# Attention pair loop: value product into its own pair, later key blocks summed before one product, tail copies one unit earlier

## The reference, cut to what matters

```python
z = jnp.einsum('bhtd,bhsd->bhts', qb, kb) * scale
mask = (s_idx[None, :] < t_idx[:, None]) & (s_idx[None, :] >= pad)
log_beta = jax.nn.log_sigmoid(z)
log_rest = jnp.where(mask, jax.nn.log_sigmoid(-z), 0.0)
later = lax.cumsum(log_rest, axis=3, reverse=True) - log_rest
att = jnp.where(mask, jnp.exp(log_beta + later), 0.0)
out = jnp.einsum('bhts,bhsd->bhtd', att, vb)
```

## Time and profile before

| what | us |
|---|---|
| median of three runs | 1735.72 |
| the profiled execution | 1740.51 |
| its span, first to last instruction | 1738.4 |
| TensorE busy in the span | 1616.3 |
| a steady pair of attention (156.15 to 189.67) | 33.52 |
| the last pair (290.21 to 326.92) | 36.71 |

### The profile page before, as it was taken

One profiled execution on the slowest core, in us unless ns is written; L12 is line 12 of the kernel. 1 busy time (PEld: TensorE's weight loads), 2 busy tenths in 40 slices (PEclk: granted clock), 3 DMA queues, 4 the chain that ended last, 5 costly groups with the idle time before them and its releaser, 6 DMA issues. The chain is left out here.

```text
span 1738.4 us, 35740 instructions
## 1 busy us (share of the span) xinstructions
PE 1616.3 (93%) x16180; PEld 1459.7 (84%) x16180; DVE 810.9 (47%) x1098; ACT 610.9 (35%) x827; POOL 162.9 (9%) x186
## 2 busy tenths in 40 slices
PE   4999998899999999979999979888669999999997
PEld 3999987899999999979998968887438888888885
DVE  3455445154442344456766535445485444334432
ACT  2445435242221222236567332233243333122321
POOL 2001001001100011300000321101030010001100
PEclk9999999799999999998999979999889999999998
DMA  3221120122332233332222110000103333323331
GB/s 100 68 62 44 56 64 30 49 86 87 97 105 78 86 89 103 97 116 79 81 70 60 45 52 4 5 4 4 49 22 87 95 90 112 91 86 97 96 99 49
DMA packets 214167, 121.35 MB, mean 70 GB/s; under 512 B 8744, under 2 KB 209600, under 8 KB 213760
## 3 DMA queue, kind: packets, MB, share of 16 engines
q1 hardware_dynamic: 213712, 118.98, 23.3%
q10 hardware_dynamic: 304, 0.08, 0.0%
HBM read 112.29 MB, written 6.76 MB: 68 GB/s over the span
## 5 line engine op out<-in xcount | busy, mean ns | idle before, releaser
L125 ACT ACTIVATE w_hi<-w_raw 128x1024 fp32r<-128x1024 f32 (+1 forms) x194 | 215.9, 1114 | 600.0 <-PE psg L732 481.0
L732 PE MATMUL psg<-x_hi,w_hi 128*128 128x264 f32 (+1 forms) x1096 | 357.2, 326 | 9.3 <-PEq L2469 9.3
L732 PE MATMUL psg<-x_lo,w_hi 128*128 128x264 f32 (+1 forms) x1096 | 357.2, 326 | 0.0
L732 PE MATMUL psg<-x_hi,w_lo 128*128 128x264 f32 (+1 forms) x1096 | 356.4, 325 | 0.0
L129 DVE TENSOR_TENSOR w_lo<-w_raw,w_hi 128x1024 fp32r<-128x1024 f32 (+1 forms) x194 | 250.4, 1291 | 145.5 <-ACT w_hi L125 145.5
L732 PEld LDWEIGHTS psg<-x_hi,w_hi 128*128 128x128 f32 x1096 | 206.2, 188 | 28.8 <-issue 10.3
L732 PEld LDWEIGHTS psg<-x_lo,w_hi 128*128 128x128 f32 x1096 | 206.2, 188 | 18.1 <-issue 0.2
L732 PEld LDWEIGHTS psg<-x_hi,w_lo 128*128 128x128 f32 x1096 | 206.6, 189 | 17.5
L732 PE MATMUL psg<-mid_hi,w_hi 128*128 128x264 f32 (+1 forms) x451 | 146.5, 325 | 0.0
L732 PE MATMUL psg<-mid_lo,w_hi 128*128 128x264 f32 (+1 forms) x451 | 146.3, 324 | 0.0
L732 PE MATMUL psg<-mid_hi,w_lo 128*128 128x264 f32 (+1 forms) x451 | 145.9, 323 | 0.0
(11 more groups left out here) (367 smaller groups left out, 3370.6 us busy)
## 6 DMA issues: line engine op xcount, KB each, us to landing
w_raw<-in_w_ffn_in_dram SPq DMA_DIRECT2D x88, 512.0 KB, 3.8
w_raw<-in_w_ffn_out_dram SPq DMA_DIRECT2D x32, 704.0 KB, 4.6
w_raw<-in_w_qkv_dram SPq DMA_DIRECT2D x24, 512.0 KB, 3.7
w_raw<-in_w_rkv_dram SPq DMA_DIRECT2D x24, 512.0 KB, 3.8
w_raw<-in_w_o_attn_dram SPq DMA_DIRECT2D x8, 512.0 KB, 4.1
w_raw<-in_w_o_rwkv_dram SPq DMA_DIRECT2D x8, 512.0 KB, 3.8
v_first<-v_pair SPq DMA_DIRECT2D x8, 264.0 KB, 2.1
res_kept<-res SPq DMA_DIRECT2D x1, 2112.0 KB, 7.8
```

The lines of the kernel that those rows point to most:

```text
L125: k.nc.scalar.activation(k.w_hi[j][:, 0:kt, :], k.raw[j][:, 0:kt, :], ACT.Copy).then_inc(k.hi_ready[j].h, 1)
L732: done = k.nc.tensor.matmul(k.psg[:, 2 * j + c, 0:size], w[:, t, :], x, start=t == first and n == 0, stop=t == last and n == 2)
```

## The change

In the attention: the product of v (unit 3p+2) moves from the previous pair's gaps to just behind `z(p)`, so each pair computes its own v; q and k of the next pair move one and two places back, with the second half of k right before the next `z`. All units from 2 on use one pair of PSUM banks. `later` is split: `own_block` is the triangular part; the cross part (`later_blocks`) no longer multiplies every pair of blocks. Instead VectorE adds the later key blocks' log-rests up in place, from the last block backwards (`later_keys`: 16, 144 and 272 columns, each waiting for the one before), ScalarE and VectorE split these sums (864 columns) into high and low (`sums_high`, `sums_low`), and TensorE makes four cross products per head, high and low. VectorE's and ScalarE's programs are reordered to match. In the tail, ScalarE's copies move from behind m = 5 to behind m = 4.

```diff
     def banks(self, i):
-        if i == 2:
-            return k.psx[:, 2, 0:HALF], k.psg[:, 2, 0:HALF]
         return k.psg[:, 3, 0:HALF], k.psx[:, 3, 0:HALF]
...
+        def sums_high(p, hp):
+            act.wait_ge(self.add_r.h, 3 * (2 * p + hp + 1))
+            if p:
+                act.wait_ge(self.later_d.h, 2 * (p - 1) + hp + 1)
+            nc.scalar.activation(b.sum_hi[hp][:], b.rest[hp][:, 512:SCORES], ACT.Copy).then_inc(self.shi_r.h, 1)
...
         for p in range(PAIRS):
-            unit_hi(k, act, 3 * p + 4, KT)
+            unit_hi(k, act, 3 * p + 3, KT)
...
             rest_high(p, 1, 1)
-            if not last:
-                unit_hi(k, act, 3 * p + 5, KT)
+            sums_high(p, 0)
+            sums_high(p, 1)
+            unit_hi(k, act, 3 * p + 4, KT)
             attend(p, 0)
             attend(p, 1)
             if not last:
-                unit_hi(k, act, 3 * p + 6, KT)
+                unit_hi(k, act, 3 * p + 5, KT)
...
+        def later_keys(p, hp):
+            n = 2 * p + hp
+            at = [piece_cols(a).start for a in (1, 3, 4, 5)]
+            dve.wait_ge(self.rlo_far.h, n + 1)
+            for step, (to, width, skip) in enumerate(((2, 16, 128), (1, 144, 128), (0, 272, 128))):
+                if step:
+                    dve.wait_ge(self.add_r.h, 3 * n + step)
+                own = b.rest[hp][:, at[to] + skip:at[to] + skip + width]
+                nc.vector.tensor_tensor(own, own, b.rest[hp][:, at[to + 1]:at[to + 1] + width], ALU.add)\
+                    .then_inc(self.add_r.h, 1)
+
+        def sums_low(p, hp):
+            dve.wait_ge(self.shi_r.h, 2 * p + hp + 1)
+            nc.vector.tensor_tensor(b.sum_lo[hp][:], b.rest[hp][:, 512:SCORES], b.sum_hi[hp][:].bitcast(F32),
+                                    ALU.subtract).then_inc(self.slo_r.h, 1)
...
-        unit_lo(k, dve, 3, KT)
-        evict(2, 0)
-        evict(2, 1)
         for p in range(PAIRS):
-            unit_lo(k, dve, 3 * p + 4, KT)
+            unit_lo(k, dve, 3 * p + 3, KT)
             clip(p, 0, 0)
...
             softplus(p, 0, 0)
+            evict(3 * p + 2, 0)
+            softplus(p, 0, 1)
+            evict(3 * p + 2, 1)
+            softplus(p, 1, 0)
+            rest_low(p, 0)
+            later_keys(p, 0)
+            softplus(p, 1, 1)
+            rest_low(p, 1)
+            later_keys(p, 1)
+            sums_low(p, 0)
+            sums_low(p, 1)
             if not last:
                 evict(3 * p + 3, 0)
...
+            unit_lo(k, dve, 3 * p + 4, KT)
             if not last:
                 evict(3 * p + 3, 1)
...
+                unit_lo(k, dve, 3 * p + 5, KT)
+                evict(3 * p + 4, 0)
...
+                evict(3 * p + 4, 1)
...
+        def later_blocks(p, hp):
+            ps = (k.psg, k.psx)[hp]
+            pe.wait_ge(self.slo_r.h, 2 * p + hp + 1)
+            for a, c in ((0, 1), (1, 3), (3, 4), (4, 5)):
+                bank, col, width, key, t0 = PIECES[a]
+                _, _, width2, _, t2 = PIECES[c]
+                at, cols = col + t2 - t0, piece_cols(c)
+                for r in (b.sum_hi[hp], b.sum_lo[hp]):
+                    done = mm(ps[:, bank, at:at + width2], b.minus[:], r[:, cols.start - 512:cols.stop - 512], start=False,
+                              stop=True, skip_group_check=True)
             done.then_inc(self.later_d.h, 1)
...
-        half(2, 0)
-        half(2, 1)
         for p in range(PAIRS):
             fill = p < PAIRS - 1
             z(p)
+            half(3 * p + 2, 0)
+            half(3 * p + 2, 1)
             if fill:
                 half(3 * p + 3, 0)
+            own_block(p, 0)
+            own_block(p, 1)
+            later_blocks(p, 0)
+            later_blocks(p, 1)
+            if fill:
                 half(3 * p + 3, 1)
-                half(3 * p + 4, 0)
-            later(p, 0)
-            later(p, 1)
-            if fill:
-                half(3 * p + 4, 1)
             turn_v(p)
             if fill:
-                half(3 * p + 5, 0)
+                half(3 * p + 4, 0)
             values(p)
             if fill:
-                half(3 * p + 5, 1)
+                half(3 * p + 4, 1)
...
-            if m == 5:
+            if m == 4:
                 act.wait_ge(self.turned.h, 1)
                 for g in range(GROUPS):
                     nc.scalar.activation(b.tok[:, g, 0:D // 2], k.psx[:, g, :], ACT.Copy).then_inc(self.copied.h, 1)
```

More of the change, by code:

```diff
@@ L200, in __init__ @@
          self.xl_r, self.sq_r, self.acc_r, self.sum_d, self.rs_r, self.half_d, self.half_r, self.z_d, self.clip_r,
-         self.exp_r, self.ln_r, self.rest_r, self.rhi_r, self.rlo_near, self.rlo_far, self.later_d, self.att_r, self.vt_d,
+         self.exp_r, self.ln_r, self.rest_r, self.rhi_r, self.rlo_near, self.rlo_far, self.later_d, self.whole_r, self.add_r, self.shi_r, self.slo_r, self.att_r, self.vt_d,
          self.vt_r, self.out_d, self.ohi_r, self.olo_r, self.v_saved) = (
@@ L205, in __init__ @@
                 "sum", "rstd", "half", "half_read", "z", "clipped", "exp", "ln", "rest", "rest_hi", "lo_near", "lo_far",
-                "later", "att", "v_turned", "v_tok", "out", "o_hi", "o_lo", "v_saved"))
+                "later", "read", "summed", "sums_hi", "sums_lo", "att", "v_turned", "v_tok", "out", "o_hi", "o_lo", "v_saved"))
     def memory(self):
@@ L223, in memory @@
         b.rest_hi, b.rest_lo = ([area.tile(f"rest_{x}{n}", [P, SCORES], F32R) for n in range(2)] for x in ("hi", "lo"))
+        b.sum_hi, b.sum_lo = ([area.tile(f"sum_{x}{n}", [P, SCORES - 512], F32R) for n in range(2)] for x in ("hi", "lo"))
         b.att = b.rest
@@ L298, in scalar @@
         nc.scalar.activation(k.rstd[:], k.rstd[:], ACT.Exp, scale=-0.5).then_inc(self.rs_r.h, 1)
-        unit_hi(k, act, 3, KT)
         def exponent(p, hp, which):
@@ L441, in vector @@
             softplus(p, 0, 0)
+            evict(3 * p + 2, 0)
[9 more added lines that the diff above has]
+            sums_low(p, 1)
             if not last:
                 evict(3 * p + 3, 0)
-            softplus(p, 0, 1)
+            unit_lo(k, dve, 3 * p + 4, KT)
             if not last:
                 evict(3 * p + 3, 1)
[L447 to L454, removed]
             dve.wait_ge(self.vt_d.h, p + 1)
@@ L458, in vector @@
             if not last:
-                unit_lo(k, dve, 3 * p + 6, KT)
-                evict(3 * p + 5, 0)
+                unit_lo(k, dve, 3 * p + 5, KT)
+                evict(3 * p + 4, 0)
             dve.wait_ge(self.ohi_r.h, p + 1)
@@ L465, in vector @@
             if not last:
-                evict(3 * p + 5, 1)
+                evict(3 * p + 4, 1)
     def gpsimd(self, pool):
@@ L537, in half @@
                 pe.wait_ge(k.lo_ready[i % 2].h, i // 2 + 1)
-                if i > 2:
-                    pe.wait_ge(self.half_r.h, i)
-            elif i > 2:
+                pe.wait_ge(self.half_r.h, i)
+            else:
                 self.wait_freed(pe, i - 1)
@@ L551, in z @@
             self.wait_freed(pe, 3 * p + 1)
-            if p == 0:
-                self.wait_freed(pe, 2)
             for bank, col, width, key, t0 in PIECES:
@@ L565, in z, with own_block @@
                 done.then_inc(self.z_d.h, 1)
-        def later(p, hp):
+        def own_block(p, hp):
             ps = (k.psg, k.psx)[hp]
@@ L643, in tensor @@
             z(p)
+            half(3 * p + 2, 0)
+            half(3 * p + 2, 1)
             if fill:
                 half(3 * p + 3, 0)
+            own_block(p, 0)
[3 more added lines that the diff above has]
+            if fill:
                 half(3 * p + 3, 1)
+            turn_v(p)
+            if fill:
                 half(3 * p + 4, 0)
-            later(p, 0)
-            later(p, 1)
+            values(p)
             if fill:
                 half(3 * p + 4, 1)
-            turn_v(p)
-            if fill:
-                half(3 * p + 5, 0)
-            values(p)
-            if fill:
-                half(3 * p + 5, 1)
     def run(self):
```

## The result

| | before | changed |
|---|---|---|
| median of the timed runs | 1739.86 us (1735.57 to 1746.88) | 1761.88 us (1753.6 to 1764.99) |
| ratio, 95% interval | | 1.0104 [1.007, 1.0137]; in a second comparison 1.0113 [1.0059, 1.0166] |
| profiled execution (span) | 1740.5 (1738.4) | 1764.4 (1762.6) |

The forecast was 1722 us, faster. By the ratios the change makes the kernel 1.0 to 1.1% slower, some 18 to 20 us; the medians of the two comparisons lie 22 and 20 us apart. Ratios leave slow executions out; of all executions here only one, of E6, was slow: 2009 us at a granted clock of 0.74.

The account below looks back on a forecast made before the run. TensorE was taken to bound the steady pairs, latency the last pair. Terms -4.15+0.8-4.3-7.05 = -14.7 gave 1725.8 us profiled, 1721.0 as median, 1722 with half a clock dip; range 1712 to 1733.

Parts of the forecast that it names:

- First z: Before pair 0: z follows k's eviction instead of the value product, starting at 51.46 instead of 55.61, -4.15 us.
- half dip: Half a clock dip, a dip being 2.80 us, added for the new gap before pair 0, bringing 1721.0 to 1722.
- Cross blocks: Steady pairs: four cross products instead of ten take 1.05 us a head instead of 2.42, saving 2.74 a pair.
- Wait before z: Seven further pairs: z now waits for the eviction of k', 0.66 us each.
- Last pair: Last pair of heads: V runs inside it, 32.4 us at half clock instead of 36.71, -4.3 us.
- Tail: Tail: copies behind unit 4 remove TensorE's wait and bring the transposes 7.05 us earlier; at least 4.1 stays.
- The chain that comes in: Steady pairs: three dependent VectorE adds before head 1's softplus take 1.03 us with waits, priced by nearest row widths.
- bounds for the adds: VectorE's three adds: between three times the 16-column row, 0.51+0.12 us, and three times the 264-column row, 1.26+0.12.
- The new gaps and the clock: Steady pairs: TensorE idles 1.86 us between own blocks and 0.66 before z; the forecast included no clock loss there.
- rival 1: Steady pairs: new gaps cost clock; dips in all pairs, 1742 us, 6%; two to four, 1728 to 1733; some, 16%.
- two signs of being wrong: Steady pairs: period under 33 or over 34.5 us, or granted clocks under 1 inside them.
- The net of the steady pairs: Steady pairs: -0.55 for the shorter work +0.66 for the wait before z, +0.1 a pair, +0.8 us for seven.

Follow-up runs that it names:

- E6: E1 with 15 useless products of 264 columns filling the wait between the two heads' own blocks; 1731.94 us, ratio 0.9938.
- E9: The changed kernel run once more, nothing altered; 1760.35 us, ratio 1.0113.
- E1: The changed kernel with GpSimd waiting for VectorE's adds of head 0 before head 1's near subtraction; 1747.2 us, ratio 1.0036.
- E7: The changed kernel with the cross blocks computed as before from single blocks, sums still made but unused, all waits kept; 1813.34 us, ratio 1.0411.
- E8: E1 with its own projection work reordered, q half 1 covering the wait between the own blocks, nothing added; 1716.97 us, ratio 0.9858.
- E10: The changed kernel with 21 useless products of 264 columns between the own blocks, GpSimd untouched; 1733.95 us, ratio 0.9949.
- E3: The changed kernel without adds and sums, with the ten cross products and head order of before; V move and tail stay; 1727.95 us, ratio 0.9935.
- E4: The kernel before with only the sums, adjacent own blocks and four cross products a head; V and tail as before; 1766.12 us, ratio 1.0153.
- E2: The kernel before with only the tail copies moved to unit 4; 1732.92 us, ratio 0.9962.
- E5: The kernel before plus sums, both waits covered by projection work, V one pair ahead, GpSimd late, tail edit; 1714.0 us, ratio 0.9845.

## Why the prediction was wrong

By its own clock the forecast was 1725.8 for the profiled execution, and 1764.4 came. The steady pairs make 19.3 of the 38.6, the unchanged stages 19.4, all other terms together less than 0.3. That the 19.4 comes from the change is not shown: most of it is within the spread of single runs (E9). The step that failed is the one on the steady pairs: the sum had +0.8 for all seven and nothing for lost clock in them, and they took 20.1 more than before, 6.6 by the longer pair at full clock (34.45 for 33.51) and 13.5 by half clock.

- **First z**: 51.46 forecast, 51.59 seen. Right; the wait there is 2.2. The half dip added for it fits too: of the eight profiles with this wait, four have 3.4 us of half clock at its end (E1, E7, E8, E10) and four have none, the first of the changed kernel among them.
- **Cross blocks**: 1.05 a head forecast, 1.09 seen (108.47 to 109.56). Right.
- **Wait before z**: 0.66 forecast, 0.62 seen, and no clock lost behind it (E3). Right.
- **Last pair**: 32.4 forecast, 32.20 seen. Right in size only, and by luck: I took half clock throughout, the granted clock was 0.79. The slow third add makes head 1's own block start at t=17.44 instead of 16.5, and with the clock back for part of them, the transposes and values took 6.00 (332.51 to 338.51) instead of 7.07. Without the sums the pair is 29.45 (E3).

```profile
323.75 0.76 PE L594 MATMUL psx<-rest_hi,tri 128*128 128x512 f32 x1 [3.02 <-DVE rest_lo L417]
...
332.51 0.74 PE L617 MATMUL psx<-ident,v_pair 128*128 128x128 f32 x5 [1.56 <-ACT rest L331]
```

- **Tail**: -7.05 forecast, -6.8 seen. Right.
- **The chain that comes in**, "1.03, by the row nearest to each width". Right for head 1 (0.99), wrong for head 0 (1.97). The widths were priced well (174, 307 and 441 ns for 0.17, 0.30 and 0.44, together the estimated 0.92 us); that GpSimd's subtraction would run beside the third add was not looked at, though the row of rest_hi that releases it could be placed in time. Worth 0.98 a pair (E1), near 7 us. Without it the undisturbed pair is 33.48 (E1), and 33.61 was forecast. The waits of 0.25 and 0.05 for the low sums don't show in the list of waits; the first crosses start 1.91 behind the own block (106.56 to 108.47), 0.15 more than the 1.76 of the earlier trace rows. My bounds for the adds, 1.38 at the top, did not hold it either, because they asked only about width.

  The Trainium skill has the rule that I passed over: "SBUF — State Buffer", section "SBUF: two separate sides", says that VectorE with two inputs from SBUF and a GpSimd operation that reads SBUF exclude each other over whole instructions, the later one standing still. The trace agrees: the add of 272 columns started at 101.99, behind GpSimd's subtraction (101.70), which ended at 103.12; the add ended at 103.41, 0.29 us later.
- **The new gaps and the clock.** This is the step that failed most. Of rival 1, dips in all pairs had 6%, and two to four dips another 16%; the forecast itself held that the clock stays full. The argument against it, that "full 128-row products stand before and behind it", is refuted: such products stand on both sides in E1, E4 and E7 and the clock fell. Of its two gaps the shorter is harmless (E3), the longer is what costs (E6, E10). In the first profile five of seven pairs fell, in the second all. A dip was priced at 2.80; in the first profile they cost 1.5 to 4.5 (35.98 and 38.92 against 34.46), 13.5 us and 20.6 us in all. Of the two signs of being wrong the clock under 1 came; the period of 34.46 stayed just under the other, 34.5.
- **The net of the steady pairs** was forecast at +0.1 a pair: nearly all of what the sums saved went back into the wait for the chain. That sentence was right and should have decided it. There was nothing to gain in these pairs, and a new gap of 1.86 us in the middle of dense work to lose by, with a row of half clock behind 1.58 us in hand.

The parts by themselves: the tail -6.6 (E2), V moved some -5 beyond that (E3 against E2), the sums +26 (E4). The sums with their waits covered, and V left where it was, are worth -19 to -20 (E5 against E2, by medians and by ratios).

## What to carry to other kernels

Work taken off a saturated TensorE is gained only if no wait takes its place; before pricing the products saved, find for each new dependent step what TensorE executes meanwhile, and put independent work there first, even useless work, as E6 and E10 did. When a short dependent chain is moved onto one engine, list what runs on the engine beside it in those microseconds, not only how long each step is alone. A profile taken once can hit or miss the clock dips, so read the granted clock of every repetition of the loop before you believe in its period.

## What the runs showed of the hardware that was not expected

- Waits of 1.69 us (E1) and 2.66 us between dense 128-row products were followed, in most pairs, by 3.4 to 17.1 us at half clock; waits of 0.62 us never were (E3, all seven pairs). The same program, run again, lost the clock in five pairs and then in seven. In a steady pair no wait between 0.62 and 1.69 us was tried.
- The 2.2 us wait before the first z ended in 3.4 us of half clock in four of eight profiles: whether a wait of this length costs anything is not the same from run to run.
- Unneeded products in a wait cost nothing here and kept the clock: pairs took 33.48 to 33.51 with 15 of them (E6) and 33.48 without (E1, its one pair at full clock), and 80 in the last pair raised its clock from 0.59 to 0.94.
- One VectorE add of 272 columns took 1416 ns beside a GpSimd subtraction, 1407 to 1416 in all eight pairs, and 441 without it; GpSimd's took 1.42 us instead of 1.28.
- Stages with exactly the same instructions took 524 to 550 us from run to run, at granted clocks from 0.94 down to 0.89.
